# Where the early tiles' lower halves, the weighted one-hots and 60 row jobs of a PEER mixer are made

## The reference, cut to what matters

```python
# xt: the 1024 normed tokens of width 1024; idx, g: the 128 picked experts of each token and their weights
def block(args):
    xc, ic, gc = args
    h = jnp.einsum('td,ted->te', xc, jnp.take(u, ic, axis=0))
    a = jax.nn.gelu(h, approximate=False) * gc
    return jnp.einsum('te,ted->td', a, jnp.take(v, ic, axis=0))
```

## Time and profile before

| | us |
|---|---|
| median of 3 runs | 3083.79 |
| lowest and highest | 3082.13, 3088.96 |
| the profiled execution, its own time | 3081.31 |
| its span, from the first to the last instruction | 3079.6 |
| spread (barrier to barrier) | about 1057.6 to 1588.6 |
| experts | about 1589 to the end |

### The profile page before, as it was taken

How to read it: one execution, slowest core, us unless ns; L and a number is a source line. 1 busy time by engine, 2 the same in 40 slices (tenths; PEclk the granted TensorE clock), 3 DMA queues, 4 the chain that set the end, 5 groups by cost and what they waited for, 6 DMA issues and landing times. The chain is left out here.

```text
span 3079.6 us, 46779 instructions
## 1 busy us (share of the span) xinstructions
PE 2968.7 (96%) x17450; PEld 1663.7 (54%) x17450; DVE 2313.1 (75%) x4663; ACT 977.5 (32%) x1417; POOL 1257.6 (41%) x883
## 2 busy tenths in 40 slices
PE   7989998989999799999999999999999999999999
PEld 4445465455555577777765555555555544444444
DVE  3255376358888666666649999989999999999996
ACT  4332365134433344444432222222222222222221
POOL 1013121014243311211226666676666666566562
PEclk9999899999999899999999999999999999999999
DMA  3110100121211245545568989989999888888884
GB/s 101 55 55 15 55 1 28 62 74 63 83 56 61 93 166 198 189 176 199 188 227 290 310 302 329 316 303 315 307 308 322 290 312 296 303 298 299 300 299 168
DMA packets 258490, 601.37 MB, mean 195 GB/s; under 512 B 21025, under 2 KB 127665, under 8 KB 255281
## 3 DMA queue, kind: packets, MB, share of 16 engines
q1 hardware_dynamic: 181168, 321.78, 31.0%
q0 software_dynamic: 73728, 268.47, 24.3%
q10 hardware_dynamic: 3456, 9.44, 0.8%
HBM read 516.78 MB, written 82.84 MB: 195 GB/s over the span
## 5 line engine op out<-in xcount | busy, mean ns | idle before, releaser
L238 PE MATMUL f_y<-f_v_hi,f_a_hi 128*128 128x512 f16 x1536 | 582.4, 379 | 8.7 <-DVE p_h L2323 8.7
L239 PE MATMUL f_y<-f_v_lo,f_a_hi 128*128 128x512 f16 x1536 | 582.1, 379 | 0.0
L240 PE MATMUL f_y<-f_v_hi,f_a_lo 128*128 128x512 f16 x1536 | 582.1, 379 | 0.0
L2292 POOL DMA_INDIRECT x_rows<-in_peer_v,p_row_index x256 | 305.9, 1195 | 281.6 <-DVE p_h L2342 256.2
L2292 POOL DMA_INDIRECT x_rows<-in_peer_u,p_row_index x251 | 321.7, 1282 | 186.4 <-DVE x_rows L2332 141.9
L2332 DVE SCALAR_TENSOR_TENSOR x_rows<-x_rows,p_xs 128x1024 f32<-128x1024 f32 x256 | 378.4, 1507 | 24.7 <-DMA x_rows<-in_peer_u,p_row_index 24.5
L2342 DVE SCALAR_TENSOR_TENSOR p_h<-x_rows,f_row_a,p_h 128x1024 f32<-128x1024 f32 x256 | 384.5, 1502 | 16.6 <-DMA x_rows<-in_peer_v,p_row_index 11.4
L2301 POOL TENSOR_TENSOR f_v_lo<-f_v_in,f_v_hi 128x1024 f16<-128x1024 f32 x128 | 286.8, 2241 | 87.4 <-ACT f_v_hi L2240 85.4
L2323 DVE SCALAR_TENSOR_TENSOR p_h<-f_y,p_h 128x512 f32<-128x512 f32 x384 | 262.4, 683 | 75.9 <-PE f_y L240 75.4
L238 PE MATMUL f_hid<-p_act_hi,x_u_hi 128*128 128x384 f16 x880 | 286.9, 326 | 2.1 <-DVEq L2308 2.1
L240 PE MATMUL f_hid<-p_act_hi,x_u_lo 128*128 128x384 f16 x880 | 286.9, 326 | 0.0
(11 more groups left out here) (314 smaller groups left out, 5489.5 us busy)
## 6 DMA issues: line engine op xcount, KB each, us to landing
f_v_in<-in_peer_v SPq DMA_DIRECT2D x128, 512.0 KB, 5.6
dense_weights<-e_stage SPq DMA_DIRECT2D x24, 2048.0 KB, 7.6
f_g_in<-dense_weights SPq DMA_DIRECT2D x32, 1536.0 KB, 16.2
x_u_in<-in_peer_u SPq DMA_DIRECT2D x56, 512.0 KB, 6.2
x_gel<-early_tiles SPq DMA_DIRECT2D x72, 384.0 KB, 3.5
e_u_in<-in_peer_u SPq DMA_DIRECT2D x48, 512.0 KB, 4.1
early_tiles<-e_gel SPq DMA_DIRECT2D x48, 384.0 KB, 2.3
a_w_in<-in_w_in SPq DMA_DIRECT2D x24, 512.0 KB, 3.7
```

The costliest lines, as they stand in the source:

```text
L238: pe.matmul(out, a_hi, b_hi, start=first, stop=False)
L239: pe.matmul(out, a_hi, b_lo, start=False, stop=False)
L240: return pe.matmul(out, a_lo, b_hi, start=False, stop=last)
L2292: nc.gpsimd.indirect_dma_start(out=rows[q % ROWS][:], out_offset=None, in_=table, in_offset=bass.IndirectOffsetOnAxis(ap=T.row_index[:, ti ...
```

## The change

Four things change in the spread, and one in the stage behind it.

- ScalarE no longer writes `u_all`. VectorE makes `u_lo` in one operation from the bank and `u_hi` (`low_from_bank`), behind `left` of step 4m for tile m. The next `turn` now waits for `u_lo_done`.
- GpSimd no longer makes `u_lo` in this stage.
- `left` of both halves of the weights is one operation of 1024 elements for one partition, where it was two of 512. The weights' halves lie in one tensor `w` for it.
- 60 of the 512 row jobs are done by VectorE in the spread, one behind the `left` of about every third step, and GpSimd fetches 65 rows there from the stage's start on: five at once, each other one when a buffer is free.
- In the experts' stage `jobs_before` spreads the other 308 jobs of the late tiles (368 before) over the same 52 steps: 5.9 for each in place of 7.1. The jobs of the last 72 steps stay.

```diff
@@ -1339,7 +1339,7 @@
 EARLY_S = 4
 EARLY_RING = 2
 ROWS = 5
-SPREAD_JOBS = 0
+SPREAD_JOBS = 60
 BLOCK = 64
 NBLOCK = DSEQ // BLOCK
 TB = 32
@@ -1354,7 +1354,7 @@
 
 
 
-    def __init__(self, nc, io, T, S, ring, first, count):
+    def __init__(self, nc, io, T, S, ring, first, count, from_bank=False):
         self.nc, self.T, self.ring = nc, T, ring
         rows = io.peer_u[0, first * P:(first + count) * P, :]
         self.u_rows = rows.rearrange("(c b p) d -> c b p d", b=ring, p=P)
@@ -1362,7 +1362,8 @@
         self.u_in = [S.sb(f"u_in{b}", [P, D]) for b in range(ring)]
         self.u_hi = [S.sb(f"u_hi{b}", [P, KT, P], F16) for b in range(ring)]
         self.u_lo = [S.sb(f"u_lo{b}", [P, KT, P], F16) for b in range(ring)]
-        self.u_all = S.sb("u_all", [P, KT, P])
+        self.u_all = None if from_bank else S.sb("u_all", [P, KT, P])
+        self.from_bank = from_bank
         self.gel = [S.sb(f"gel{b}", [P, DSEQ]) for b in range(ring)]
         self.u_ps = S.ps("u_ps", [P, KT, P])
         self.hid = [S.ps(f"hid{b}", [P, HALF])[:, 0:DHALF] for b in range(2)]
@@ -1402,7 +1403,7 @@
 
     def turn(self, pe, c, b):
         pe.wait_ge(self.u_loaded[b], c * 16 + 16)
-        pe.wait_ge(self.u_all_done, BASE + c * self.ring + b)
+        pe.wait_ge(self.u_lo_done if self.from_bank else self.u_all_done, BASE + c * self.ring + b)
         for k in range(KT):
             last = pe.transpose(self.u_ps[:, k, :], self.u_in[b][:, k * P:(k + 1) * P], self.T.ident[:])
         last.then_inc(self.u_turned, 1)
@@ -1422,6 +1423,18 @@
         pool.wait_ge(self.u_all_done, BASE + n + 1)
         self.nc.gpsimd.tensor_tensor(self.u_lo[b][:], self.u_all[:], self.u_hi[b][:],
                                      ALU.subtract).then_inc(self.u_lo_done, 1)
+
+    def split_high(self, act, c, b):
+        n = c * self.ring + b
+        act.wait_ge(self.u_turned, n + 1)
+        act.wait_ge(self.hid_done, BASE + 2 * (n - self.ring) + 2)
+        self.nc.scalar.activation(self.u_hi[b][:], self.u_ps[:], ACT.Copy, scale=S_U).then_inc(self.u_hi_done, 1)
+
+    def low_from_bank(self, dve, c, b):
+        n = c * self.ring + b
+        dve.wait_ge(self.u_hi_done, n + 1)
+        self.nc.vector.scalar_tensor_tensor(self.u_lo[b][:], self.u_ps[:], S_U, self.u_hi[b][:], ALU.mult,
+                                            ALU.subtract).then_inc(self.u_lo_done, 1)
 
     def hidden(self, pe, c, b, half):
         n = c * self.ring + b
@@ -1832,7 +1845,7 @@
     STEPS = BLOCK // BANK_T
     with ExitStack() as ctx:
         S = Space(nc, ctx, "e")
-        E = EarlyTiles(nc, io, T, S, EARLY_RING, N_RETRIEVE, EARLY_S * NBLOCK)
+        E = EarlyTiles(nc, io, T, S, EARLY_RING, N_RETRIEVE, EARLY_S * NBLOCK, from_bank=True)
 
         def ring_at(blk, b):
 
@@ -1844,7 +1857,9 @@
         same = [S.sb(f"same{r}", [P, P, BANK_T], F16) for r in range(2)]
         left = [S.sb(f"left{r}", [P, 2, P, BANK_T], F16) for r in range(RING)]
         right = [S.sb(f"right{r}", [P, BANK_T, P], F16) for r in range(RING)]
-        key2, w_hi, w_lo = (S.sb(n, [P, DSEQ], F16) for n in ("key2", "w_hi", "w_lo"))
+        key2 = S.sb("key2", [P, DSEQ], F16)
+        w = S.sb("w", [P, 2, DSEQ], F16)
+        w_hi, w_lo = w[:, 0, :], w[:, 1, :]
         stage = [S.sb(f"stage{b}", [P, NKEYS, TB]) for b in range(2)]
         tab = [S.ps(f"tab{r}", [P, BANK_T, P]) for r in range(RING)]
         vec_step = S.sem("vec_step")
@@ -1869,6 +1884,7 @@
         @block.vector
         def _(dve):
             c = Chain(dve, vec_step)
+            dve.sem_inc(E.u_lo_done, BASE)
             c.step(nc.vector.tensor_scalar(w_t, w_t, S_G, None, ALU.mult))
             c.step(nc.vector.tensor_copy(iota[:], lanes(T.iota[:], 2, P, P, BANK_T)))
             c.link(nc.vector.tensor_copy(key2[:], key2_t))
@@ -1894,8 +1910,11 @@
                 nc.vector.tensor_tensor(right[r][:], lanes(T.iota[:], 1, P, BANK_T, P),
                                         lanes(key1_t[:, toks], 2, P, BANK_T, P), ALU.is_equal)
                 dve.wait_ge(same_done, n + 1)
-                nc.vector.tensor_tensor(left[r][:, 0], same[s % 2][:], each(w_hi), ALU.mult)
-                nc.vector.tensor_tensor(left[r][:, 1], same[s % 2][:], each(w_lo), ALU.mult).then_inc(built, 1)
+                nc.vector.tensor_tensor(left[r][:], lanes(same[s % 2][:], 1, P, 2, P, BANK_T),
+                                        lanes(w[:, :, toks], 2, P, 2, P, BANK_T), ALU.mult).then_inc(built, 1)
+
+                if n % 4 == 0 and n // 4 < EARLY_S * NBLOCK:
+                    E.low_from_bank(dve, *ring_at(n // 4 // EARLY_S, n // 4 % EARLY_S))
                 for q in range(SPREAD_JOBS * n // ALL, SPREAD_JOBS * (n + 1) // ALL):
                     row_job(q)
             for b in range(2):
@@ -1967,12 +1986,12 @@
                     if s in HALVES:
                         b, half = HALVES[s]
                         if half == 0 and b + 1 < EARLY_S:
-                            E.split(act, *ring_at(blk, b + 1))
+                            E.split_high(act, *ring_at(blk, b + 1))
                         elif half == 0 and not last:
-                            E.split(act, *ring_at(blk + 1, 0))
+                            E.split_high(act, *ring_at(blk + 1, 0))
                         E.gelu(act, *ring_at(blk, b), half)
 
-            E.split(act, 0, 0)
+            E.split_high(act, 0, 0)
             with act.Fori(0, NBLOCK - 1) as blk:
                 step(blk, False)
             step(NBLOCK - 1, True)
@@ -1986,7 +2005,6 @@
 
         @block.gpsimd
         def _(pool):
-            E.prime_gpsimd(pool)
 
             def fetch(q):
                 if q >= ROWS:
@@ -1996,14 +2014,8 @@
                     in_offset=bass.IndirectOffsetOnAxis(ap=T.row_index[:, 0, q:q + 1], axis=0)).then_inc(
                         row_loaded[q % ROWS], 16)
 
-            BLOCKS_TILES = EARLY_S * NBLOCK
-            fetched = 0
-            for n in range(BLOCKS_TILES):
-                E.low(pool, *ring_at(n // EARLY_S, n % EARLY_S))
-                upto = SPREAD_JOBS * (n + 1) // BLOCKS_TILES + ROWS if SPREAD_JOBS or n + 1 == BLOCKS_TILES else 0
-                for q in range(fetched, upto):
-                    fetch(q)
-                fetched = max(fetched, upto)
+            for q in range(SPREAD_JOBS + ROWS):
+                fetch(q)
             for b in range(ROWS):
                 pool.wait_ge(row_loaded[b], 16 * (SPREAD_JOBS // ROWS + 1))
```

## The result

The changed kernel takes 3066.82 us (3062.3 to 3068.61, 4 runs) against 3085.21 in the same comparison, a ratio of 0.9941 with a 95% interval of 0.9926 to 0.9957: 18.2 us, from 13 to 23. In a second comparison it was 0.995 (0.9932 to 0.9967), 15 us.

A forecast was written before the change was run, and what follows sets the result against it. PE (TensorE) was taken to bound spread and experts. Start -3.9, clock -0.5, steady spread 0, experts -2.1 and -0.5 sum to -7.0 us: 3083.79 to 3076.8 us, range 3069 to 3085.

The forecast's parts named there:

- The bound: Spread and experts: PE is busy nearly throughout, so work taken off other engines returns only what PE waits for them.
- VectorE's sum: Steady spread: VectorE needs 8.74 us a tile, 9.98 with its wait, under PE's 10.47, so cost 0.
- 60 to 90 us of slack: Spread: VectorE's wait for PE's table matmuls gets smaller but stays present, 60 to 90 us.
- Rivals 1 and 3: Spread: combined product loses the double rate, +12 us, chance 0.07; a fetch blocks VectorE, +11 us, chance 0.03.
- The start: Start of the spread: the 4.15 us wait before `hidden` falls away, `turn` starts 0.3 later: about -3.9 us.
- Rival 2: First five fetches take bandwidth from tiles 0 and 1, experts keep PE's waits: -2.7 us, 3081.1, chance 0.23.
- Rival 4: Change is idle: VectorE's wait for `u_hi` eats more, PE waits as at the start: 0, 3084, chance 0.05.
- The clock: Start of the spread: less half-speed work without the pause, bounds 0 and -2.5 us, taken -0.5.
- The experts: PE's waits for VectorE's additions shrink: -2.1 us up to 2460 us, -0.5 after, bounds -2.5 and -1.7.
- My own sign of being wrong: PE waits for VectorE's products or lower halves in the steady spread, or the experts gain much more than 4 us.
- The run of four jobs ahead of the product: Experts: this run of row jobs, one at 3.41 us, stays but starts earlier; rival 2 has it keep PE's waits.
- The range: Forecast's own range -10.9 to -4 us, 3071 to 3081 with scatter; full range 3069 to 3085.

The follow-up runs named there:

- the first profile: The kernel before, profiled ahead of the experiments: 3081.31 us; the second profile is that kernel unchanged, run again: ratio 1.0003.
- kernels with idle operations: The changed kernel plus eight or five unneeded `right` comparisons on VectorE ahead of tile 0's lower half: eight 0.9962 of the kernel before, five not timed in turns.
- the profile of the pair: The changed kernel's first profile, 3062.3 us; the second is the changed kernel unchanged, run again: ratio 0.995 to the kernel before.

## Why the prediction was right in kind and too small

- **The bound.** Right: TensorE sets the spread and the experts, and the steady spread takes 487.8 us, from the 100th matmul to the experts' first transpose, in every kernel whose end was left alone (502.1 to 502.2 to X, or 503.8 to 503.9 with the end's slow matmuls). VectorE's 2.3 us more in a tile cost nothing, since it still waits 70 us.
- **VectorE's sum.** Right: 0.68 us for the product, 1.22 for the row job, 1.21 for the lower half, with pitches of 0.60, 1.14 and 1.13. The forecast of 60 to 90 us of slack held. Rivals 1 and 3 are out: the double rate stays, and a fetch does not block VectorE. None of the 60 row jobs of the spread meets a fetch, since one is issued when a job ends, for 0.94 us; the 48 products that do have a median of 680 ns, and the 155 row jobs of the experts that do take 1.22 us at most.
- **The start.** Right: -3.9 forecast, -4.0 measured. Rival 2's delay of tile 0 by the first fetches did not show: TensorE waits 4.8 to 5.3 us for its rows in the ten kernels that issue five fetches at the start, and 4.9 to 5.2 in the three that do not. Rival 4 is out too.
- **The clock, taken as -0.5.** Mis-sized: -1.4 and -1.7, together -3.1. The first part was within my bounds of 0 to -2.5: 7 hidden matmuls at half speed in place of 16. It stays gained when a pause of 5.5 us is put ahead of the transpose (the old two are 1.2 and 4.2), so it goes with where the pause stands. The second part was put at nothing: I had not seen that the end of the spread has a pause too, behind which 16 upper-half matmuls have a mean of 366 ns in place of 326. The kernels with idle operations show that such a term comes and goes with small shifts in time and doesn't need the old engines' work; a range should hold it on both sides.
- **The experts, -2.6 of at most -4.2.** Mis-sized, and this is the step that failed. I took bounds from the waits of one execution (2.5, and 1.7 for the longest), measured by the profile's idle time, and then less than the bound: 2.1 and 0.5. Up to matmul 14900 the changed kernel is 5.3 us ahead of the first profile and 7.0 ahead of the second. The longest wait went whole, 1.8 us where I had 0.5, and the others cost 3.4 to 5.1 us with what each gives back beyond its idle time. Another 0.5 us came ahead of matmul 10000, where my windows had a hole: between the barrier and 1640 us TensorE waited 1.5 us for VectorE's lower half, now 1.0. My own sign of being wrong, more than 4 us from the experts, came in. The same program has 8.7 or 10.7 us of waits for additions, and the changed one without the jobs 11.6; 60 jobs bring them down to between 4.1 and 5.8, whichever kernel they stand in. The run of four jobs ahead of the product, which I thought would keep some of them, keeps none up to 2443 us in the profile of the pair and one of 0.4 us in the second.
- **The range.** Its lower bound was mis-added: 3.9, 2.5, 2.5 and 1.7 are 10.6, not 10.9. Even that is short of what was timed.
- **The rest.** My terms corrected in this way, -4.0, -3.1, -5.8 and +0.7, are the 12.2 of the profiles. The timed 15 to 18 us have intervals that begin at 10 and 13. Nothing in the profiles from S on accounts for more than 14.4, and ahead of S they scatter by 13.6 us. What part of the 3 to 6 us between is chance, and what part a difference ahead of S, stays open.

## What to carry to other kernels

Moving work off an engine that is not the bound can still pay by the short waits it causes on the one that is; read their size from more than one execution, and match the starts of the same matmuls rather than add up idle time, since the sum of many waits near zero slack moves by a quarter between runs of the same program. Once they are gone, further unloading brings nothing: try half and one and a half times the amount to see where that is. And where an early pause of TensorE is removed, look at the clock behind every other pause.

## What the runs showed of the hardware

- After pauses of TensorE of 1.9 to 2.4 us in the later part of the program 5 to 11 hidden matmuls at half speed follow or don't, at some 1.6 us each time with the transposes between; after 3.6 and 5.3 us at the barrier 10 and 15 followed, 1.5 and 2.3 us. Behind the same pause of 2.4 us, shifts of the same program by 1.7 or 4 us at one place changed that 500 us later.
- GpSimd's subtraction of 128x1024 took 5.88 us with VectorE busy beside it for 3.90, 3.98 with VectorE busy for 2.00, and 2.14 in the steady spread of the kernel before with VectorE idle.
- A row job takes 1.22 us by itself or beside a fetch's issue, 3.40 where GpSimd's subtraction starts 0.17 us behind it, and 3.06 where it starts 0.15 us ahead. With 60 jobs fewer in the experts none takes more than 3.07; with none or 30 moved the longest take 3.41.
